# A hybrid decoder layer on one core: the bounded difference of the decays' sums moves from VectorE to ScalarE, and its loads move one chunk forward in the order

## The chip, the cores and the metric

The kernel runs on 1 core of one Trainium2 chip. The metric is the device time in microseconds (us) of the whole kernel. TensorE is called PE below, VectorE DVE, ScalarE ACT, GpSimd POOL, and SyncE, whose queue issues all DMAs, SP.

## The reference, cut to what matters

One layer: an RMSNorm, one input projection for all branches, a differential attention, a gated short convolution and a Mamba-2 scan (SSD), then an output projection and a last RMSNorm. 1024 tokens and 16 meta tokens, model width 1024, all in float32. The change touches the scan alone:

```
adt  = a * dt                                  # per head, 16 heads in 4 groups of R = 4
acum = cumsum(adt) inside a chunk of 128       # "sums of the decays"
seg  = acum[..., :, None] - acum[..., None, :]
lmat = exp(where(causal, seg, -inf))           # 128 x 128 for each head and chunk
y_diag = (C B^T * lmat) @ (x * dt)             # inside the chunk
y_off  = (C @ state) * exp(acum)               # from the chunks before
state  = state * exp(acum[-1]) + B^T (decay_s * x * dt)
```

The kernel forms `lmat` transposed: keys on the 128 partitions, queries along the free axis. It doesn't mask `seg` before the exponential; it bounds the difference at 0 (for a query after the key the difference is never above 0), and the causal triangle is multiplied in afterwards, together with C B^T.

## The kernel before, in words

The work is cut into four iterations, one for each group of heads: the order `BODY` for the first three and `LAST` for the fourth, with a prologue `AHEAD` in front and the output projection behind (from 887 us on). An order is a list of steps with their argument, written by `schedule()` (L185 to L337). Every engine walks the same list and carries out its own part of a step; SP does the DMAs of a step. Nothing else orders the work: each engine runs its instructions in the order of the list, and semaphores hold it back where it needs another engine.

An iteration has an attention part and a scan part. In the scan part the loop of L303 goes over c = 1 to 11. In round c stand, in this order: `chunk c`; `norm c-2`; a fifth of the round's filler; `scan c-1`; `carry c`; `decay c+1`; three fifths of the filler; `ssm_out c-2`; the last fifth. The filler is independent PE work that is dealt over the rounds: steps `project` (PE, 12 matmuls for each half of a piece), `piece` (the copy of a finished piece out of its PSUM bank), `load` (a tile of w_in, by SP), `split` (that tile into a high part by ACT, L991 to L994, and a low part, by POOL at L904 and for a half of two tiles by DVE at L1286), and the short convolution. Pieces use PSUM banks 0 and 1 in turn, so PE can begin piece n+2 only when ACT or DVE has emptied the bank of piece n. The steps `z 1` to `z 8` (PE L1800, 24 matmuls each) use the same two banks: ACT makes a tanh (L1105), DVE multiplies (L1465) and frees the bank. `z 4` stands in front of `chunk 0` and `decay 1`; `z 5` stands in round 1, and `z 6` to `z 8` behind `decay 2`.

What the steps of the scan do:

- `decay a`. SP (L780 to L787) loads the sums of four heads for chunk a, broadcast to all partitions (256 KB), into one of two halves of `acum_b`. It waits until the difference of chunk a-2 is formed (semaphore `seg_ok`), and for a = 1 also for stores of an earlier step. DVE (L1428 to L1435) waits for that load (`acum_in`) and for `scan a-2` (`scan_done`, as the matrices of chunk a-2 lie in the same half of `lm_buf`), and makes four `tensor_scalar` (L1433, 128x128 each: subtract the key's own sum, take the minimum with 0). ACT (L1099 to L1101) waits for `seg_ok` and makes one exponential over 128x512 in place, which counts `l_ok`.
- `chunk a`. PE turns x and B and forms C B^T (L1785). DVE makes x*dt (L1445), x*d (L1448), the masked C B^T (L1451), a copy of B (L1452), and then, once `l_ok` and `scan a-1` are there, the product with `lmat` (L1456, which counts `g_ok`). POOL makes one more product (L919).
- `scan a`. PE: four matmuls with `lmat` (L1814), the part from the state (L1816), the new state (L1820). DVE: state (L1474), three steps of y (L1477 to L1481), the gated y (L1485).
- `norm a` and `ssm_out a`. ACT squares y (L1110), DVE takes the mean (L1492), POOL the power (L895), ACT scales y (L1112), PE turns it (L1584), ACT copies it out (L1119).

In `LAST` the filler also holds `out_load 0` to `3` (SP L792 to L807: two loads each for the output projection). `out_load 0` stands in round 6 and waits until the last tile of w_in is split (`w_lo_ok`, L796); `out_load 1` stands in round 7, in front of `scan 6` and `decay 8`.

Of the kernel before, what the change touches and what calls it, by code (L numbers as in the profile page):

```python
# [11 lines left out]
ALU = mybir.AluOpType  # L12
# [172 lines left out]
def schedule(last):  # L185
    out = []

    def add(name, arg=0, d=0):
        if not (last and d):
            out.append((name, arg, d))  # L190

    def emit(unit):
        for name, arg, d in unit:
            if name in ("load", "split"):
                add(name, arg % NT, d + arg // NT)
            else:
                add(name, arg, d)

    def filler(units, jobs, slots):
        state = [0, 0.0]  # L200

        def fill(weight=1.0):
            state[1] += weight
            while state[0] < len(units) and state[0] < len(units) * state[1] / slots - 1e-9:

                while jobs and jobs[0][0] <= state[0] - 7 and not (last and jobs[0][1][0] == "conv"):
                    emit([jobs.pop(0)[1]])
                emit(units[state[0]])
                state[0] += 1

        def spare(n):
            while n > 0 and jobs and jobs[0][0] <= state[0]:
                emit([jobs.pop(0)[1]])
                n -= 1
        return fill, spare

    units, jobs = half_pieces([TXS0, TXS1, TB, TC, TG], 0)
    fill, spare = filler(units, jobs, sum(ATT_FILL))

    def t_sums(s, at):  # L220

        a, n = divmod(3 * (s - 3) + at, 8)
        if s < 3 or a >= T_PAIRS:
            return
        if n == 0:
            add("t_load", a)
        elif 3 <= n < 7:
            add("t_sum", (a, n - 3))
        elif n == 7:
            add("t_store", a)  # L230

    for s in range(QB + 1):
        f = [ATT_FILL[s] * w for w in (ATT_SPLIT if s < QB else ATT_LAST)]
        if s < QB:
            add("scores", (s, 0))
        fill(f[0])
        t_sums(s, 0)
        if s < QB:
            spare(ATT_SPARE[0])
        if s == 0:  # L240
            add("turn_v")
        if s >= 1:
            add("turn", s - 1)
        if s == QB:
            add("split", TZ1)
            add("load", TCB)
            add("load", TCC)
            add("attn_out", 0)
        if s < QB:
            add("exp", (s, 0))  # L250
        fill(f[1])
        t_sums(s, 1)
        if s < QB:
            add("scores", (s, 1))
            add("exp", (s, 1))
        if s >= 1:
            add("values", s - 1)
        if s == 5:
            add("o_mean", 0)
        if s < QB:  # L260
            spare(ATT_SPARE[1])
        if s < QB:
            add("mix", s)
        if s == 6:
            add("o_scale", 0)
        fill(f[2])
        t_sums(s, 2)
        if s < QB:
            spare(ATT_SPARE[2])

    add("o_mean", 1)
    add("z", 1)
    spare(1)
    add("o_scale", 1)
    add("z", 2)
    spare(2)
    add("z", 3)
    add("attn_out", 1)
    add("store_attn")
    spare(9)  # L280
    add("z", 4)
    add("chunk", 0)
    add("decay", 1)
    units = [[("z", a, 0)] for a in range(5, QB + 1)]
    units[-1].append(("split", TCB, 0))
    units += [[]] * PAUSE
    conv, jobs = half_pieces([TCB, TCC, TCH, TGC], 0)
    jobs = [(n + len(units), job) for n, job in jobs]
    if last:
        for n in range(len(conv)):  # L290
            if ("split", TGC, 0) in conv[n]:
                for j in range(EARLY):
                    conv[n + j].append(("out_load", j, 0))
                conv[-5].append(("out_slot", 0, 0))
                conv[-2].append(("out_slot", 1, 0))
                break
        units += conv
        jobs.pop()
    else:
        units += conv + half_pieces([TQ, TK, TV], 1)[0]  # L300
    slots = LAST_FILL if last else SCAN_FILL
    fill, spare = filler(units, jobs, sum(slots))
    for c in range(1, CH + 3):  # L303
        f = [slots[c - 1] * w for w in SCAN_SPLIT]
        if c < CH:
            add("chunk", c)
        if 1 <= c - 2 < CH:
            add("norm", c - 2)
        if last and c == CH + 1:
            spare(9)  # L310
            for j in range(EARLY, KS):
                add("out_load", j)
            add("conv", 4)
            add("out_slot", 3)
            add("out_slot", 4)
        fill(f[0])
        if not (last and c == CH):
            spare(SCAN_SPARE[0])
        if c - 1 < CH:
            add("scan", c - 1)  # L320
            if 0 < c < CH - 1:
                add("carry", c)
        if c + 1 < CH:
            add("decay", c + 1)
        fill(f[1])
        if not (last and c == CH):
            spare(SCAN_SPARE[1])
        if 1 <= c - 2 < CH:
            add("ssm_out", c - 2)
        fill(f[2])  # L330
        spare(SCAN_SPARE[2])
        if c == CH and last:
            add("out_slot", 2)
            add("out_begin", 0)
    add("store_ssm")
    spare(9)
    return out  # L337
# [46 lines left out]
def build(nc, x, meta_tokens, norm_w, w_in, w_out, attn_lambda, attn_norm_w, sconv_w, ssm_conv_w,  # L384
# [6 lines left out]
    with ExitStack() as ctx:  # L391
# [322 lines left out]
        def _(eng):  # L714
# [24 lines left out]
            def iteration(i, steps):  # L739
                for step, a, d in steps:  # L740
# [36 lines left out]
                    elif step == "conv" and a == 4:  # L777
                        eng.wait_ge(convg_ok, it + 2)
                        eng.dma_start(y_dram[bass.ds(it * P + HEADS * P, P), :], conv_y[:, :]).then_inc(convg_st, 16)
                    elif step == "decay":  # L780

                        eng.wait_ge(seg_ok, it * QB + max(a - 2, 0) + 1)
                        if a == 1:
# [169 lines left out]
        def _(eng):  # L953
# [24 lines left out]
            def iteration(i, steps):  # L978
                for step, a, d in steps:
# [114 lines left out]
                    elif step == "values":  # L1094
# [2 lines left out]
                        eng.wait_ge(o_sq, it * QB + a + 1)  # L1097
                        eng.activation(o_squares, o_n[:, a, :], ACT.Square, accum_out=o_ss[:, a:a + 1]).then_inc(o_sq, 1)
                    elif step == "decay":  # L1099
                        eng.wait_ge(seg_ok, it * QB + a + 1)  # L1100
                        eng.activation(lmat[:, a % 2, :, :], lmat[:, a % 2, :, :], ACT.Exp).then_inc(l_ok, 1)  # L1101
                    elif step == "z":
                        p = PZ + a - 1
                        eng.wait_ge(piece_done, it * PPI + p + 2)
                        eng.activation(th_piece[:, p % 2, 0:GW], pb[p % 2][:, 0:GW], ACT.Tanh, scale=0.5).then_inc(zth_ok, 1)  # L1105
                    elif step == "norm":
                        n = it * QB + a
                        eng.wait_ge(y_gated, n + 1)
                        eng.wait_ge(z_ms_ok, n)
                        eng.activation(th_tile[:, 0:GW], y_n[:, a % 2, :], ACT.Square, accum_out=z_ss[:, a % 2:a % 2 + 1]).then_inc(z_sq, 1)  # L1110
                        eng.wait_ge(z_rs_ok, n)
                        eng.activation(y_n[:, a % 2, :], y_n[:, a % 2, :], ACT.Copy, scale=z_rs[:, a % 2:a % 2 + 1]).then_inc(y_n_ok, 1)  # L1112
                    elif step == "ssm_out":
                        n = it * QB + a
                        eng.wait_ge(y_tr, n + 1)
                        if a == 1:
                            eng.wait_ge(ssm_st, it * 32 + 16)
                        for t in range(2):
                            ins = eng.activation(ys[:, t, (a - 1) * P:a * P], yt_ps[:, t * P:(t + 1) * P], ACT.Copy, scale=par_sn[:, t:t + 1])  # L1119
                        ins.then_inc(ys_ok, 1)  # L1120
                    elif step == "out_slot":
                        if a >= 3:
                            eng.wait_ge(piece_done, HEADS * PPI + 1)
                        slot_free(a)
                        high_y(a)
                        high_w(a)
# [46 lines left out]
        def _(eng):  # L1173
# [18 lines left out]
            def iteration(i, steps):  # L1192
                for step, a, d in steps:
# [218 lines left out]
                    elif step == "conv":  # L1412
# [11 lines left out]
                        else:  # L1424
                            for b in range(2):
                                eng.wait_ge(bank_free[b], it * (PPI // 2) + (PPI + 1 - b) // 2 + 1)
                            eng.scalar_tensor_tensor(conv_y[:, :], conv_y[:, :], 0.5, conv_g[:, META:L], ALU.mult, ALU.mult).then_inc(convg_ok, 1)
                    elif step == "decay":  # L1428

                        eng.wait_ge(acum_in[a % 2], it * 64 + 16 * ((a + 1) // 2))  # L1430
                        eng.wait_ge(scan_done, it * CH + max(a - 1, 0) + 1)
                        for r in range(R):
                            ins = eng.tensor_scalar(lmat[:, a % 2, r, :], acum_b[:, a % 2, r, :], sg[:, 1, a, r:r + 1], 0.0,  # L1433
                                                    ALU.subtract, ALU.min)
                        ins.then_inc(seg_ok, 1)  # L1435
                    elif step == "chunk":

                        n = META if a == 0 else P
# [430 lines left out]
```

## Time and profile before

| | us |
|---|---|
| median of 3 runs (lowest, highest) | 1050.74 (1050.49, 1052.12) |
| the profiled execution: its time | 1049.79 |
| the profiled execution: its span, first to last instruction | 1048.1 |
| PE busy in the span | 1013.8 (97%) |
| DVE busy | 665.6 (64%) |
| ACT busy | 401.8 (38%) |
| POOL busy | 253.8 (24%) |
| scan part of the first head group | about 162 to 275 |
| scan part of the last head group | about 795 to 887 |

The granted clock of PE is 0.998 of full speed over the span. "Busy" counts the time in which an instruction of the engine runs; what is missing to the span is idle time. Of the 16,326 instructions 128 are the four differences of 32 decay steps, and 32 are their exponentials.

### The profile page before, as it was taken

The page shows a single profiled execution, that of the slowest core. Times are in us where ns is not written, and L with a number is a line of the kernel's source. Part 1 is how long each engine was busy: PE and PEld are TensorE (multiplying, and loading weights), DVE is VectorE, ACT ScalarE, POOL GpSimd, SP SyncE. Part 2 cuts the span into 40 slices and gives each one's busy share as a digit, 9 for nine tenths or more (in the row PEclk, how much of TensorE's full clock was granted, in tenths as well). Part 3 has the DMA queues.
Part 4 walks back from the last instruction along what each step waited for, and adds up shares of the span by engine and source line. Part 5 has one row for each costly group of instructions (what it writes and reads, how often), then busy time and mean ns, then how long its engine had stood idle before and what let it go on. Part 6 is the DMA issues. An engine that isn't in the chain of part 4 may idle for free.

```text
span 1048.1 us, 16326 instructions
## 1 busy us (share of the span) xinstructions
PE 1013.8 (97%) x6177; PEld 924.9 (88%) x6177; DVE 665.6 (64%) x1327; ACT 401.8 (38%) x892; POOL 253.8 (24%) x222
## 2 busy tenths in 40 slices
PE   4999999999999999999999999999999999999996
PEld 3889989898999898989999989899999898888885
DVE  7555767557257674672576756724767646798866
ACT  6333442233444332334343222343442233544554
POOL 3012331333223312332224133222241330000002
PEclk9999999999999999999999999999999999999999
DMA  8012322221142222211422322114223203994313
GB/s 268 1 44 81 101 81 71 71 61 44 47 133 101 71 81 71 61 41 41 141 84 76 93 71 61 42 41 141 76 70 101 71 20 105 359 389 140 100 51 161
DMA packets 105945, 101.22 MB, mean 97 GB/s; under 512 B 6022, under 2 KB 79852, under 8 KB 105868
## 3 DMA queue, kind: packets, MB, share of 16 engines
q1 hardware_dynamic: 105868, 100.18, 30.0%
q8 instruction: 50, 0.82, 0.3%
q14 instruction: 27, 0.22, 0.1%
HBM read 79.11 MB, written 21.05 MB: 96 GB/s over the span
## 4 chain that ended last, share of the span: by engine, by line
PE 84%; DVE 7%; issue 3%; DMA 2%; ACT 2%; POOL 1%; SPq 0%; POOLq 0%; DVEq 0%; ACTq 0%
PE ps L1599 43%; PE ps L1608 13%; PE ps L1800 9%; PE ps L1584 5%; PE ps L1765 3%; DVE lm_buf L1433 2%; PE ps L1814 2%; DMA acum_b<-acum_scratch 2%; PE ps L1743 2%; PE ps L1744 2%; PE ps L1816 1%; PE ps L1820 1%; PE ps L1691 1%; PE ps L1766 1%; DMA conv_u<-in_norm_w 1%
## 5 line engine op out<-in xcount | busy, mean ns | idle before, releaser
L1599 PE MATMUL ps<-u_hi,w_hi 128*128 128x348 f32 (+3 forms) x1024 | 364.4, 356 | 6.7 <-ACT conv_b_s L1053 2.5
L1599 PE MATMUL ps<-u_lo,w_hi 128*128 128x348 f32 (+3 forms) x1024 | 348.3, 340 | 0.0
L1599 PE MATMUL ps<-u_hi,w_lo 128*128 128x348 f32 (+3 forms) x1024 | 347.7, 340 | 0.0
L1599 PEld LDWEIGHTS ps<-u_hi,w_hi 128*128 128x128 f32 x1024 | 194.0, 189 | 19.8 <-issue 5.5
L904 POOL TENSOR_TENSOR w_lo<-w_raw,w_hi 128x1024 fp32r<-128x1024 f32 (+1 forms) x56 | 123.1, 2197 | 346.2 <-ACT w_hi L994 274.4
L1599 PEld LDWEIGHTS ps<-u_hi,w_lo 128*128 128x128 f32 x1024 | 193.3, 189 | 10.9
L1599 PEld LDWEIGHTS ps<-u_lo,w_hi 128*128 128x128 f32 x1024 | 193.7, 189 | 10.3
L895 POOL TENSOR_TENSOR small<-small,m_half 128x1 f32<-128x1 f32 (+2 forms) x57 | 41.5, 729 | 338.9 <-DVE small L1545 144.8
L1372 DVE TENSOR_REDUCE small<-ps 128x1 f32<-128x144 f32 (+7 forms) x64 | 49.5, 774 | 95.8 <-PE ps L1747 95.3
L1800 PE MATMUL ps<-w_hi,u_hi 128*128 128x256 f32 x256 | 73.1, 286 | 0.0
L1800 PE MATMUL ps<-w_lo,u_hi 128*128 128x256 f32 x256 | 72.0, 281 | 0.0
L1800 PE MATMUL ps<-w_hi,u_lo 128*128 128x256 f32 x256 | 72.0, 281 | 0.0
L1086 ACT ACTIVATE work<-ps,small 128x144 f32<-128x144 f32 (+7 forms) x64 | 48.0, 751 | 53.7 <-DVE small L1372 53.7
L1584 PE MATMUL ps<-ident,work 128*128 128x128 f32 (+2 forms) x369 | 56.6, 288 | 6.1 <-DVE work L1208 6.1
L1608 PE MATMUL ps<-q_hl 128*128 128x512 f32 x264 | 62.1, 389 | 0.0
L1433 DVE TENSOR_SCALAR lm_buf<-acum_b,sg 128x128 f32<-128x128 f32 x128 | 44.5, 409 | 27.5 <-DMA acum_b<-acum_scratch 27.5
L1101 ACT ACTIVATE lm_buf<-lm_buf 128x512 f32<-128x512 f32 x32 | 20.2, 632 | 107.0 <-DVE lm_buf L1433 107.0
L1112 ACT ACTIVATE y_n<-y_n,small 128x256 f32<-128x256 f32 x32 | 16.3, 510 | 112.9 <-POOL small L895 112.9
L1608 PEld LDWEIGHTS ps<-q_hl 128*128 128x128 f32 x264 | 49.6, 188 | 10.3
L1584 PEld LDWEIGHTS ps<-ident,work 128*128 128x128 f32 (+2 forms) x369 | 44.4, 143 | 9.9 <-DVE work L1208 7.8
L1456 DVE TENSOR_TENSOR lm_buf<-lm_buf,cbm 128x512 f32<-128x512 f32 x32 | 22.6, 707 | 43.3 <-PE ps L1820 43.1
L994 ACT CAST w_hi<-w_raw 128x1024 fp32r<-128x1024 f32 x48 | 49.9, 1040 | 0.1
(302 smaller groups left out, 1768.7 us busy)
## 6 DMA issues: line engine op xcount, KB each, us to landing
w_raw<-in_w_in SPq DMA_DIRECT2D x56, 512.0 KB, 4.1
acum_b<-acum_scratch SPq DMA_DIRECT2D x32, 256.0 KB, 4.4
acum_b<-in_w_out SPq DMA_DIRECT2D x22, 256.0 KB, 4.3
work<-in_w_out SPq DMA_DIRECT2D x16, 256.0 KB, 4.0
t_scratch<-work SPq DMA_DIRECT2D x16, 256.0 KB, 2.3
t_scratch<-acum_b SPq DMA_DIRECT2D x16, 256.0 KB, 2.6
y_scratch<-ys SPq DMA_DIRECT2D x8, 512.0 KB, 4.0
work<-in_x SPq DMA_DIRECT2D x4, 1024.0 KB, 8.4
```

The costliest lines, as they stand in the source:

```text
L895: return eng.tensor_tensor(to[0:rows_, n:n + w], of[0:rows_, n:n + w], m_half[0:rows_, 0:w], ALU.pow)
L904: eng.tensor_tensor(w_lo[:, a % 2, ks, :], w_raw[:, a % 2, ks, :], w_hi[:, a % 2, ks, :].bitcast(F32), ALU.subtract).then_inc(w_lo_ok, 1)
L994: eng.copy(w_hi[:, b, :, :], w_raw[:, b, :, :]).then_inc(w_hi_ok, 1)
L1086: eng.activation(prob[m][:, 0:nk], s_ps[:, 0:nk], ACT.Exp, bias=mx[:, m:m + 1], accum_out=psum_e[:, s % 2, m:m + 1]).then_inc(exp_ok, 1)
L1372: eng.tensor_reduce(mx[:, m:m + 1], s_ps[:, 0:nk], AX.X, ALU.max, negate=True).then_inc(max_ok, 1)
L1433: ins = eng.tensor_scalar(lmat[:, a % 2, r, :], acum_b[:, a % 2, r, :], sg[:, 1, a, r:r + 1], 0.0, ALU.subtract, ALU.min)
L1456: eng.tensor_tensor(lmat[:, b, :, :], lmat[:, b, :, :], cbm[:, b, :].unsqueeze(1).to_broadcast([P, R, P]), ALU.mult).then_inc(g_ok, 1)
L1584: return eng.transpose(dst, src, ident[0:n, 0:n])
L1599: ins = eng.matmul(dst, w[:, k, 0:m], u[:, k, cols], start=(k == 0 and n == 0), stop=(k == KD - 1 and n == 2))
L1608: ins = eng.matmul(ps[:, BANKS[n // KS][t], :], y[:, at], w, start=(begins and m == 0), stop=(ends and m == 2), skip_group_check=True)
L1765: eng.matmul(o_ps[:, P:2 * P], a_t[:, n, :], v_blk[:, n, :], start=(n == 0), stop=False)
L1800: ins = eng.matmul(pb[p % 2][:, 0:GW], u[:, k, ca:cb], w[:, :, k, :], start=(k == 0 and n == 0), stop=(k == KD - 1 and n == 2))
```

## The change

The step `decay` is cut in two. Its load becomes a step `decay_load`, which only SP carries out, with the same waits. Loads 1 and 2 stand in front of `z 4`; load c+1 stands at the head of round c, from c = 2 to 7, in front of `chunk c` and of all the round's filler. So load a stands in front of the filler of round a-1 instead of behind its first fifth and behind `scan a-2`.

The four differences become ACT's. The sums' load and `scan a-2` are now waited for by ACT; it makes four activations `relu(sum of the key - sum of the query)`, with the key's sum as a bias for each partition and a scale of -1, counts `seg_ok`, waits for it, and the exponential takes a scale of -1. DVE has no part in `decay` any more. Number and size of the loads stay as they were, and so does everything else in the list.

```diff
@@ schedule()
     add("store_attn")
     spare(9)
+    add("decay_load", 1)
+    add("decay_load", 2)
     add("z", 4)
     add("chunk", 0)
     add("decay", 1)
...
     for c in range(1, CH + 3):
         f = [slots[c - 1] * w for w in SCAN_SPLIT]
+        if 1 < c and c + 1 < CH:
+            add("decay_load", c + 1)
         if c < CH:
             add("chunk", c)
@@ SyncE
-                    elif step == "decay":
+                    elif step == "decay_load":
 
                         eng.wait_ge(seg_ok, it * QB + max(a - 2, 0) + 1)
@@ ScalarE
                     elif step == "decay":
+                        eng.wait_ge(acum_in[a % 2], it * 64 + 16 * ((a + 1) // 2))
+                        eng.wait_ge(scan_done, it * CH + max(a - 1, 0) + 1)
+
+                        for r in range(R):
+                            ins = eng.activation(lmat[:, a % 2, r, :], acum_b[:, a % 2, r, :], ACT.Relu, bias=sg[:, 1, a, r:r + 1], scale=-1.0)
+                        ins.then_inc(seg_ok, 1)
                         eng.wait_ge(seg_ok, it * QB + a + 1)
-                        eng.activation(lmat[:, a % 2, :, :], lmat[:, a % 2, :, :], ACT.Exp).then_inc(l_ok, 1)
+                        eng.activation(lmat[:, a % 2, :, :], lmat[:, a % 2, :, :], ACT.Exp, scale=-1.0).then_inc(l_ok, 1)
@@ VectorE
-                    elif step == "decay":
-
-                        eng.wait_ge(acum_in[a % 2], it * 64 + 16 * ((a + 1) // 2))
-                        eng.wait_ge(scan_done, it * CH + max(a - 1, 0) + 1)
-                        for r in range(R):
-                            ins = eng.tensor_scalar(lmat[:, a % 2, r, :], acum_b[:, a % 2, r, :], sg[:, 1, a, r:r + 1], 0.0,
-                                                    ALU.subtract, ALU.min)
-                        ins.then_inc(seg_ok, 1)
```

## Rows read from the trace of the kernel before

**Rows 1.** The page: busy time (share of the span) and count of each engine.
```profile
PE 1013.8 (97%) x6177; PEld 924.9 (88%) x6177; DVE 665.6 (64%) x1327; ACT 401.8 (38%) x892; POOL 253.8 (24%) x222
```

**Rows 2.** First scan's window: length, busy us of PE, PEld, DVE, ACT, POOL, clock, DMA.
```profile
162.00:275.00 113.00, 110.84 (x703) 102.40 (x703) 68.56 (x161) 35.65 (x81) 31.73 (x31) 1.00 0.23 66
```

**Rows 3.** Waits of PE, whole span: total us, times, longest.
```profile
PE ps L1599 <- ACT conv_b_s L1053: 2.5, 3, 0.9
PE ps L1599 <- ACT conv_u L1057: 2.4, 3, 0.8
...
PE ps L1599 <- DVE conv_g L1337: 1.2, 3, 0.4
PE ps L1584 <- ACT y_n L1112: 1.2, 2, 1.0
PE ps L1814 <- DVE lm_buf L1456: 0.7, 1, 0.7
PE ps L1599 <- DVE conv_u L1334: 0.5, 1, 0.5
```

**Rows 4.** The chain of waits, first head group: start us, us, what.
```profile
197.60 4.65 DMA acum_b<-acum_scratch
...
203.71 0.58 ACT conv_b_s L1053
...
211.13 3.40 DVE lm_buf L1433 x4
...
215.56 2.16 PE ps L1599 x12
...
244.70 3.40 DVE lm_buf L1433 x4
```

**Rows 5.** Timeline of ACT, first group: start, us, engine, line [idle before it <- releaser].
```profile
196.30 1.04 ACT L994 CAST w_hi<-w_raw 128x1024 fp32r<-128x1024 f32 x1
...
210.26 1.04 ACT L994 CAST w_hi<-w_raw 128x1024 fp32r<-128x1024 f32 x1
...
225.40 0.62 ACT L1119 ACTIVATE ys<-ps,par_sn 128x128 f32<-128x128 f32 x2 [0.29 <-PE ps L1584]
```

**Rows 6.** Line 1433: ns of one (min/median/max), first and last start.
```profile
L1433 DVE TENSOR_SCALAR lm_buf<-acum_b,sg x128: 273/279/2432, 177.2 to 873.0; 128x128 f32<-128x128 f32 x128
```

**Rows 7.** Timeline of POOL, first head group.
```profile
211.37 2.48 POOL L904 TENSOR_TENSOR w_lo<-w_raw,w_hi 128x1024 fp32r<-128x1024 f32 x1 [1.56 <-ACT w_hi L994]
...
225.19 2.38 POOL L904 TENSOR_TENSOR w_lo<-w_raw,w_hi 128x1024 fp32r<-128x1024 f32 x1 [3.63 <-ACT w_hi L994]
```

**Rows 8.** Groups of ACT: busy us, mean ns of one | idle before them, releaser.
```profile
L1101 ACT ACTIVATE lm_buf<-lm_buf 128x512 f32<-128x512 f32 x32 | 20.2, 632 | 107.0 <-DVE lm_buf L1433 107.0
L1119 ACT ACTIVATE ys<-ps,par_sn 128x128 f32<-128x128 f32 x64 | 20.0, 367 | 14.8 <-PE ps L1584 14.8
...
L1112 ACT ACTIVATE y_n<-y_n,small 128x256 f32<-128x256 f32 x32 | 16.3, 510 | 112.9 <-POOL small L895 112.9
L1110 ACT ACTIVATE th_tile<-y_n 128x256 f32<-128x256 f32 x32 | 13.5, 422 | 0.1
```

**Rows 9.** Timeline of ACT, last group: the shortest idle time before an exponential.
```profile
850.22 0.63 ACT L1101 ACTIVATE lm_buf<-lm_buf 128x512 f32<-128x512 f32 x1 [1.35 <-DVE lm_buf L1433]
```

**Rows 10.** Timeline of DVE, first group, around the z steps.
```profile
177.25 0.88 DVE L1433 TENSOR_SCALAR lm_buf<-acum_b,sg 128x128 f32<-128x128 f32 x4 [1.97 <-DMA acum_b<-acum_scratch]
...
179.82 0.41 DVE L1465 SCALAR_TENSOR_TENSOR work<-th_piece,ps 128x256 f32<-128x256 f32 x1
```

**Rows 11.** The chain of waits, first group: three z steps of PE.
```profile
178.23 8.72 PE ps L1800 x72
```

**Rows 12.** The chain of waits, last group: queue of SP and the last load.
```profile
863.68 0.42 SPq L737
...
865.32 7.09 DMA acum_b<-acum_scratch
```

**Rows 13.** Groups of ACT by form: the only table load of the trace.
```profile
L1000 ACT ACT_TABLE_LOAD x1 | 1.3, 1283 | 0.8 <-PEq L1857 0.8
```

## The prediction

> **What bounds the kernel now.** I read the page's busy line first: PE is busy for 1013.8 of 1048.1 us [rows 1]. No work of another engine counts unless it makes PE wait. The change touches the four scan parts, so the window of the first of them comes next: PE lacks 113.00 - 110.84 = 2.16 us there [rows 2]. Third, the list of PE's waits says who ends such waits [rows 3]: once in each of the first three groups the copies L1053 (2.5 us for the three), L1057 (2.4) and L1337's gating (1.2), 6.1 together; in the last group y_n twice (1.0 and 0.2), L1456 once (0.7) and L1334 once (0.5), 2.4 together. That is 8.5 us in all, and a change that leaves PE's own work alone can't save more in these parts.
>
> Fourth, the chain of waits says what stood behind the copies [rows 4]. The copies themselves are short; they are queued behind the exponential of a decay step on ACT, and that waits for DVE's four differences. At the first place the differences wait for their own load: SP had been held by a load of w_in, and issued the load of the sums only behind it, at 197.60; that took 4.65 us, and the copy ended at 203.71 + 0.58 = 204.29. At the other two places the load is there, but the four differences take 3.40 us in place of 0.88 [rows 4, 10]: one of them took up to 2.432 us where the median is 0.279 [rows 6], and the row of 211.13 to 214.53 lies across POOL's L904 (211.37 to 213.85) [rows 7].
>
> **The change, part by part.**
>
> *The differences leave DVE.* 128 instructions go. Four take 0.88 us where four medians would be 1.12, so neighbours overlap by 0.08, and DVE's chain loses 0.80 us at each decay step [rows 6, 10], or 3.3 us beside L904.
>
> *They are added to ACT.* No 128x128 activation with a pointer that reads SBUF stands in the rows. L1110 has 256 columns without a pointer, 0.422 us; L1101 has 512, 0.632 [rows 8]: 0.210 us for 256 columns, so 128 columns are 0.317. A pointer costs 0.088 (L1112 against L1110, 0.510 against 0.422), which gives 0.40 us each. Two L1119 in a row (0.367 each) took 0.62 [rows 5, 8], so neighbours overlap by 0.11. Four: 4 x 0.40 less 3 x 0.11 = 1.27 us. The bounds: not below the 0.88 of DVE's four, since L1119, the nearest row, is slower than L1433; not above 4 x 0.632 = 2.53, the exponential with four times the columns. I take 1.27, from the near rows. The exponential keeps its 0.63. ACT's wait on its own count I put at nothing to 0.1 us, and inside the rounding.
>
> *What this does to ACT's order.* ACT stood idle before the exponentials for 107.0 us [rows 8], before each of the 32, 1.35 us at the least [rows 9]. It now waits itself for the load and for `scan a-2`, and both are older than DVE's result, since DVE did L1456, L1474 and the steps up to L1485 between that scan and the differences. So the 1.27 us lie in idle time, and an exponential starts earlier than before, at the tightest place by 0.08 us. Behind the waiting ACT are queued the tanh of z, the copies of pieces and the squares; all of them waited for the exponential before too.
>
> One place is late: `decay 1`, where the load arrives last (DVE waited 1.97 us for it, until 177.25 [rows 10]). There ACT's four cost 1.27 instead of 0.88, and what follows is 0.4 us later: behind the exponential DVE makes L1456 and frees the bank of `z 5`, at 179.82 + 0.41 = 180.2 before [rows 10]. PE wants that bank for `z 7`, a third of the way into its row of three, at 178.23 + 2.91 = 181.1 [rows 11]. A margin of 0.9 shrinks to 0.5: nothing is lost. DVE gains there, as it no longer stands still for the load.
>
> *The three places.* First: ACT was free at 196.30 + 1.04 = 197.34 [rows 5]. Load 4 lies there by then: its gate, the difference of `decay 2`, opens near 181, and SP meets it before the held load of w_in. So the exponential ends near 199.3 and the copy near 199.9. PE wants the bank about 0.9 before it began, near 203.5: 3.6 us to spare, and the wait goes whole. Second: ACT was free at 210.26 + 1.04 = 211.3 [rows 5]; 1.27 + 0.63 more gives 213.2, the copy (at most the other's 0.58) ends by 213.8, and PE wants it at 215.56 - 0.8 = 214.8 [rows 3, 4]: 1.0 to spare. Third: DVE's four took 3.40 us from 244.70 [rows 4]; ACT's 1.27 start no later, so the exponential and L1337 behind it come at least 2.1 us earlier, against a wait of 0.4 [rows 3]. All 6.1 us go. Late next are the bank of the second place (1.0 us) and that of `z 7` (0.5).
>
> *The last group.* The 1.0 us wait for y_n has DVE's four in its chain, without the stretch: 0.80 comes off, 0.2 stays. The 0.7 for L1456 has no decay step in its chain (w_in's split, then `chunk 2`) and stays, and so does the second wait for y_n, 0.2. The 0.5 for L1334 stood behind DVE's wait for the last load (865.32, 7.09 us [rows 12]) and goes, since DVE doesn't wait any more. But the load itself is hardly ahead: load 8 stands at the head of round 7, and `out_load 0`, in round 6, holds SP until the last tile of w_in is split. SP then issues two loads for it, the second at 863.68 [rows 12], and load 8 at about 864.1, 1.2 us earlier than before, in a crowd. ACT waits for it until 869 to 871 (the 4.65 to 7.09 us that such loads took), ends the exponential near 871 to 873, and PE wants the y_n behind it about 876: covered. Sum here 0.80 + 0.5 = 1.3 us.
>
> *The other loads.* SP carries the same 32 loads. Each now stands in front of a round's loads of w_in and could hold these, but its gate, the difference of a-2, is two rounds old. I put this at nothing; the cover is the time from a w_in load, issued next to 197.60 and some 5 us under way, to its split at 210.26 [rows 4, 5], 8 us. Loads that land earlier gain no more than the waits counted above.
>
> *The sum.* 6.1 + 1.3 = 7.4 us. For the profiled execution: span 1048.1 - 7.4 = 1040.7, time 1049.79 - 7.4 = 1042.4. The median of the runs lies 0.95 above the profiled time, so I expect 1050.74 - 7.4 = 1043.3 us.
>
> *Where rules of the skill bear on it.* That a stretched difference ran beside POOL's L904 is in the rows; that it is a lock is not. The Trainium skill (SBUF — State Buffer, on its engine and DMA ports) says that VectorE and GpSimd share one port pair, that one instruction holds it whole while the other stands still, and that ScalarE has ports of its own. By it ACT's four keep their length beside L904 and the sum stands at 7.4 us; without it the first rival holds, at 3.8. ACT's L1119 at 225.40 took 0.62 for two beside POOL's L904 of 225.19 [rows 5, 7], so by that rule the trace agrees.
>
> The same skill speaks against the move (ScalarE: Activation LUTs, Rules for kernel authors): relu, max and min are VectorE's, not ScalarE's. The rows agree so far as 0.40 us stand against 0.279; what it would do here is the fourth rival.
>
> **The rivals.**
>
> *1. The stretch follows the work.* If what stretches L1433 is traffic in memory and not a matter between DVE and POOL, ACT's four stretch too. The second place has them at 211.3, just as L904 starts (211.37 to 213.85 [rows 7]): they end near 214.9 and the copy near 216, so PE waits as before, and so at the third place. Gone are then the first place's 2.5 us [rows 3] and the last group's 1.3: 1050.7 - 3.8 = 1046.9. Against it is L1119 beside L904.
>
> *2. The waits come back elsewhere.* Drawn together, PE could meet the z banks (0.5 us of margin), y_n or the state late, and gain nothing: 1050.7. For it: the chain of y_n runs over DVE, POOL and ACT, and already costs 0.2 and 1.0. Against it: that chain starts at PE's own `scan`, so it moves forward along with PE, and DVE loses work.
>
> *3. Slower: relu isn't in the table set of the exponential.* The trace has one table load in all, 1.283 us [rows 13]; squares, exponentials, tanh and copies alternate without one, but relu isn't among them. If it forces a reload, a decay step has two, 2.57 us more, and every place with less margin decides against the change: the bank of `z 7` (0.5) comes 2.1 us late, that behind the second decay about as late again, the second place (1.0) 1.6, the third (2.1 less 0.4) 0.9. That is some 6.5 us in each of four groups, 26 us, with the 7.4 gone: 1069. Against it is the mixture above.
>
> *4. Slower: ACT's chain is on the path everywhere.* 1.27 against 0.88 in 32 steps is 12.5 us: 1063. Against it are the 1.35 us or more of idle time before each exponential.
>
> **How the numbers follow.** Forecast 0.76, first rival 0.12, second 0.07, third 0.03, fourth 0.02. The median of this kernel's runs tells 0.2%, 2.1 us, from no change. Faster is the forecast and the first rival, 0.88; same is the second, 0.07; slower 0.05. The predicted time is the forecast's, 1043.3. Below it the bound is the 8.5 us: 1042.2, and about half a us for the scatter of medians, 1041.6. Above it the first rival's 1046.9 is taken in, with the same scatter and a little: 1047.6. The upper bound of ACT's four (2.53, 1.26 more than taken) would cost 0.8 us in the z steps of each group and 0.3 at the second place, some 4 us: 1047.3, inside.
>
> **What would show each step.** L1433 gone from DVE; four new activations of 0.37 to 0.40 us at each of 32 places, a row of four in 1.2 to 1.3 us, also beside L904. PE's waits for L1053, L1057 and L1337 gone; those for y_n down to 0.4 in all; L1456's 0.7 still there. Loads 2 to 8 landed before ACT wants them, but for load 8 of the last group, issued behind two loads of `out_load 0`, where ACT waits for 3 to 6 us. One table load. The prediction is wrong if PE's missing time in the four scan parts isn't down to about 1.1 us in all, or if an exponential starts later than before at any place but `decay 1`.

## The result, and the profile after

The changed kernel takes 1040.2 us (median of 4 runs, 1040.0 to 1041.1), the kernel before in the same comparison 1050.88 (1050.49 to 1052.12): a ratio of 0.9895, with a 95% interval of 0.9881 to 0.9909. In a later comparison it stood at 1040.92 against 1050.17, 0.9913 (0.9900 to 0.9927). So the gain is 9.3 to 10.7 us. Forecast were 7.4 us, with 1041.6 as the lower end of the range: the direction was right, and the time lies below the range. Two executions among the experiments below, one of the kernel with ScalarE alone and one of that with load 8 ahead, took 2026 and 3550 us: the ratios leave them out, and without them these two medians are 1045.45 and 1040.67 instead of 1045.52 and 1040.9.

The profiled execution has a span of 1038.7 us, against 1048.1. Its busy line answers to [rows 1]:

```profile
PE 1010.6 (97%) x6177; PEld 923.9 (89%) x6177; DVE 623.7 (60%) x1199; ACT 443.3 (43%) x1020; POOL 253.9 (24%) x222
```

DVE lost 42 us and 128 instructions, and ACT gained the same 128 and 41.5 us. Look at PE: the same 6177 instructions, but 3.2 us less busy time. The prediction counted on PE's idle time alone, so this is the first sign of what it missed; it is taken up below.

PE's waits (total, times, longest), which answer to [rows 3]. The one for `work`, 1.2 us longer than before in this execution, belongs to the prologue, and so do two more of 8.6 and 2.3 us. The copies L1053 and L1057 (now L1057 and L1061), the wait for L1337 and that for L1334 are gone, y_n is down from 1.2 to 0.4, and L1456 (now L1458) keeps its 0.7, as forecast:

```profile
PE ps L1586 <- DVE work L1218: 7.3, 4, 2.6
...
PE ps L1816 <- DVE lm_buf L1458: 0.7, 1, 0.7
PE ps L1586 <- ACT y_n L1122: 0.4, 2, 0.2
```

The window of the first scan, for [rows 2] (columns as there). PE lacks nothing any more:

```profile
162.00:273.00 111.00, 111.00 (x710) 103.06 (x709) 57.54 (x130) 46.47 (x114) 32.27 (x31) 1.00 0.23 67
```

ACT's differences, from the view of their line (ns of one: min, median, max; then what ended ACT's idle time before them):

```profile
L1108 ACT ACTIVATE lm_buf<-acum_b,sg x128: 384/389/408, 177.9 to 860.4; 128x128 f32<-128x128 f32 x128
its engine sat idle before it (us, times) until:
  DMA acum_b<-acum_scratch: 15.1, 6
  PE ps L1822: 3.8, 4
```

And the second place of the prediction, ACT's timeline, with POOL's split beside it (210.83 to 213.23):

```profile
209.72 1.04 ACT L998 CAST w_hi<-w_raw 128x1024 fp32r<-128x1024 f32 x1
210.65 1.28 ACT L1108 ACTIVATE lm_buf<-acum_b,sg 128x128 f32<-128x128 f32 x4
211.96 0.64 ACT L1111 ACTIVATE lm_buf<-lm_buf 128x512 f32<-128x512 f32 x1
212.50 0.42 ACT L1061 COPY conv_u<-ps 128x342 f32<-128x342 f32 x1
```
```profile
210.83 2.40 POOL L908 TENSOR_TENSOR w_lo<-w_raw,w_hi 128x1024 fp32r<-128x1024 f32 x1 [1.56 <-ACT w_hi L998]
```

Four in 1.28 us (1.27 forecast), not stretched beside POOL, where DVE's four took 3.40 [rows 4].

**Where the time came from.** The best clock in this kernel is the start of the same PE work in each head group. These are the first three z steps of each group, in the chain of waits (start us, us, what), and the start of the output projection's steady part. First before, then after:

```profile
162.09 8.51 PE ps L1800 x72
...
373.12 8.51 PE ps L1800 x72
...
584.01 8.51 PE ps L1800 x72
...
794.87 8.52 PE ps L1800 x72
...
895.55 130.63 PE ps L1608 x576
```
```profile
162.72 8.52 PE ps L1802 x72
...
370.85 8.53 PE ps L1802 x72
...
578.97 8.52 PE ps L1802 x72
...
787.07 8.52 PE ps L1802 x72
...
886.15 130.63 PE ps L1610 x576
```

From group to group it was 211.03, 210.89 and 210.86 us, and is 208.13, 208.12 and 208.10: 8.43 us less. From the last group's z steps to the output projection it was 100.68 and is 99.08: 1.60 less. Together 10.03 us. Behind that point both take 152.55 us. In front of it the changed kernel's prologue took 0.63 us longer in this execution. The change doesn't touch the prologue, but over the executions shown here its end lies anywhere from 161.8 to 163.6, and a whole time moves with it. The distances don't: in a second trace of the changed kernel they are 208.10, 208.15, 208.12 and 99.05. So the experiments below are read by distances first. The change itself is worth 10.0 us; the idle time that left PE's list is 7.4 (8.5 less 1.1).

The same stretch, from the first group's z steps to the output projection, in the view by windows (columns as in [rows 2]), before and after:

```profile
162.09:895.55 733.46, 724.65 (x4649) 673.86 (x4648) 445.21 (x944) 258.22 (x607) 205.72 (x170) 1.00 0.25 76
```
```profile
162.72:886.15 723.43, 722.07 (x4649) 673.12 (x4648) 403.59 (x816) 299.49 (x735) 205.72 (x170) 1.00 0.25 77
```

PE's idle time falls from 8.81 to 1.36 us, by 7.45, and its busy time by 2.58 for the same 4649 matmuls. The other 0.6 of the page's 3.2 us lie in the prologue.

### The profile page after: what moved, and what is told of

Read it like the earlier page. It is cut to its first block, busy times and chain, and to the rows that moved or that the text cites. A ratio compares the mean times of both kernels' runs of the same rounds, so it can differ in the third digit from the quotient of the medians.

```text
span 1038.7 us, 16326 instructions
## 1 busy us (share of the span) xinstructions
PE 1010.6 (97%) x6177; PEld 923.9 (89%) x6177; DVE 623.7 (60%) x1199; ACT 443.3 (43%) x1020; POOL 253.9 (24%) x222
## 4 chain that ended last, share of the span: by engine, by line
PE 93%; DVE 3%; issue 1%; ACT 1%; DMA 1%; POOL 0%; POOLq 0%; SPq 0%; DVEq 0%; ACTq 0%
PE ps L1601 51%; PE ps L1610 13%; PE ps L1802 9%; PE ps L1586 5%; PE ps L1767 3%; PE ps L1816 2%; PE ps L1745 2%; PE ps L1746 2%; PE ps L1818 1%; PE ps L1822 1%; PE ps L1693 1%; PE ps L1768 1%; PE ps L1787 1%; DMA conv_u<-in_norm_w 1%; PE ps L1749 0%
## 5 line engine op out<-in xcount | busy, mean ns | idle before, releaser
L1458 DVE TENSOR_TENSOR lm_buf<-lm_buf,cbm 128x512 f32<-128x512 f32 x32 | 22.1, 691 | 50.8 <-PE ps L1822 40.4
L1802 PEld LDWEIGHTS ps<-w_hi,u_hi 128*128 128x128 f32 x256 | 48.1, 188 | 1.3 <-issue 1.3
L1108 ACT ACTIVATE lm_buf<-acum_b,sg 128x128 f32<-128x128 f32 x128 | 40.8, 391 | 19.0 <-DMA acum_b<-acum_scratch 15.1
```

Of the source, the lines that this page charges most:

```text
L1108: ins = eng.activation(lmat[:, a % 2, r, :], acum_b[:, a % 2, r, :], ACT.Relu, bias=sg[:, 1, a, r:r + 1], scale=-1.0)
L1458: eng.tensor_tensor(lmat[:, b, :, :], lmat[:, b, :, :], cbm[:, b, :].unsqueeze(1).to_broadcast([P, R, P]), ALU.mult).then_inc(g_ok, 1)
L1802: ins = eng.matmul(pb[p % 2][:, 0:GW], u[:, k, ca:cb], w[:, :, k, :], start=(k == 0 and n == 0), stop=(k == KD - 1 and n == 2))
```

## The experiments

The open question: 10.0 us came from waits that the trace gave as 7.4. **Theory:** a wait costs PE more than the idle time shown, since matmuls in a row overlap, and a wait takes that overlap away too. Compare the first place in both traces, the timeline of PE (start, us, line; an entry of several is merged), first before and then after:

```profile
203.10 0.39 PE L1785 MATMUL ps<-work 128*128 128x128 f32 x2
204.42 0.39 PE L1599 MATMUL ps<-u_hi,w_hi 128*128 128x342 f32 x1 [0.94 <-ACT conv_b_s L1053]
```
```profile
203.74 0.39 PE L1787 MATMUL ps<-work 128*128 128x128 f32 x2
203.88 0.40 PE L1601 MATMUL ps<-u_hi,w_hi 128*128 128x342 f32 x1
```

From start to start it is 1.32 us with the wait and 0.14 without: 1.18 us lost, where the trace says 0.94 idle. The other 0.24 stand in it as busy time.

**Rival A:** a wait costs its idle time, and the 2.6 us come from elsewhere. **Rival B:** they come from DVE's lighter load.

### One part at a time: the loads alone

```diff
 # the kernel before, with the change's schedule() and SP step
-                    elif step == "decay":          # SyncE
+                    elif step == "decay_load":
 # ScalarE and VectorE as before
```

> The kernel before with the loads of the sums moved forward alone; the differences stay on VectorE. Theory (a wait of PE costs its idle time in the trace and about 0.24 us more, as the start-to-start distances of the two traces say): the waits for L1053 go (3 x (0.85 + 0.24)) and that for L1334 (0.5 + 0.24), those for L1057 and L1337 stay, since the differences still lie across POOL's L904: 4.0 us, about 1046.8. Rival A (a wait costs its idle time and no more): 3.0 us, 1047.8. Rival B (the excess over the idle time came from VectorE's lighter load): 3.0 us here too, and the excess turns up in the kernel that moves the differences alone.

Measured: 1046.83 us against 1050.33 beside it, ratio 0.9966 (0.9955 to 0.9978). That interval is 1045.6 to 1048.0 us, so it holds the theory's 1046.8 and the rivals' 1047.8 alike, and the traces have to decide. PE's waits that are left in the scan:

```profile
PE ps L1603 <- ACT conv_u L1061: 2.4, 3, 0.8
...
PE ps L1603 <- DVE conv_g L1341: 1.3, 3, 0.4
PE ps L1588 <- ACT y_n L1116: 1.2, 2, 1.0
PE ps L1818 <- DVE lm_buf L1460: 0.7, 1, 0.7
```

The step between two groups is 209.87 us (373.45 to 583.32) against 210.89: 1.02 us for one wait of about 0.8 [rows 3]. Over the three groups (163.55 to 793.18) it is 3.15 us for waits of 2.5, so 0.22 more for each of the three, and with the last group 3.99 us, against 4.0 by the theory and 3.0 by the rivals. Both rivals fall here: the excess is there, though DVE's load didn't become lighter. The loads alone bring 40% of the 10.0 us.

### The other part: ScalarE alone

```diff
 # the changed kernel
-    add("decay_load", 1)
-    add("decay_load", 2)
     add("z", 4)
     add("chunk", 0)
+    add("decay_load", 1)
     add("decay", 1)
...
-        if 1 < c and c + 1 < CH:
-            add("decay_load", c + 1)
...
         if c + 1 < CH:
+            add("decay_load", c + 1)
             add("decay", c + 1)
```

> The changed kernel with the loads put back to where they stood, directly in front of the differences, which ScalarE makes. Theory: the waits for L1057 (3 x (0.8 + 0.24)), L1337 (3 x (0.4 + 0.24)), L1334 (0.5 + 0.24) and 0.8 of y_n go; the waits for L1053 stay and grow by 0.4 each, as ScalarE's four are that much longer behind the landed load: 5.4 us in all, about 1045.4. Rival A: 3.3 + 1.2 to 1.3 - 1.2, about 3.7 us, 1047.1. Rival B: 2.3 us more than rival A, 1044.8, and none of it in the first experiment.

Measured: 1045.52 us, ratio 0.9953 (0.9940 to 0.9966), 0.1 us from the theory's number (rival B's was 1044.8, rival A's 1047.1). The interval is 1044.0 to 1046.8 us: it leaves out rival A's number, but not rival B's. By the distances the gain is 3.97 us in three groups and 1.08 in the last, 5.05 together, against 5.4 by the theory and 3.7 by rival A. What is missing lies with y_n, which kept 0.8 us in three waits where 0.4 in two was expected. The wait for the copy L1053 stayed and grew from 2.5 to 3.7 for the three, by 0.4 each:

```profile
PE ps L1599 <- ACT conv_b_s L1055: 3.7, 3, 1.6
```

The two parts alone bring 3.5 and 4.8 us by their medians, 4.0 and 5.05 by the distances, and both together 10.0. Each takes waits that the other leaves, and only both together take away the late load without putting ACT's slower four behind it.

### What a wait costs: 28 waits for PE's own matmuls, and their control

```diff
 # the changed kernel, TensorE; the control waits for x_done instead of scan_done
+                    elif step == "carry":
+                        eng.wait_ge(scan_done, it * CH + a + 1)
```

> The changed kernel, and PE waits for the end of its own scan matmuls in every carry step, 28 times, before it goes on with matmuls that need nothing of them. Theory: each wait costs what lies between the usual start of the next matmul (0.35 us before the modelled end of the last one, which is 0.59 us for two of 256 columns) and the end with its signal, 0.40 to 0.45 us, of which the trace shows only 0.1 or less as idle time: 11 to 12.5 us, 1051 to 1053, with PE's missing time up by 3 us at the most. Rival A: the time grows by no more than the idle time shown, 3 us, 1043.

> The control of the drained wait: the same 28 waits at the same places, but on a count that the chunk step's matmuls gave a microsecond earlier, so the wait is met already. Theory: the pipeline isn't drained, 0 to 0.5 us, 1040.2 to 1040.7. Rival C (the wait instruction itself costs, drained or not): as much as the drained one, 1051 or more.

Measured: 1048.17 us with the drained waits, 1040.08 with the control. A wait that is met costs nothing that can be measured (rival C falls). From group to group it is 210.14 us (161.81 to 371.95) against 208.12 (162.05 to 370.17), 0.29 for each of seven, and 6.02 us for the 21 of three groups, again 0.29. In the last group it is only 1.15 us for seven, but there the two waits for y_n (0.4) are gone and L1456's is down from 0.7 to 0.4: the drained waits took their place. That the medians also differ by 28 x 0.29 = 8.1 us is chance in part, since the distances sum to 7.2. I had expected 0.40 to 0.45: I took the later start of one matmul for the cost, but the matmul behind it follows closer. The pages' busy lines decide between the theory and rival A, first the drained waits, then the control:

```profile
span 1044.9 us, 16340 instructions
...
PE 1017.4 (97%) x6177; PEld 922.3 (88%) x6177; DVE 623.5 (60%) x1199; ACT 442.7 (42%) x1020; POOL 253.5 (24%) x222
```
```profile
span 1038.0 us, 16340 instructions
...
PE 1011.3 (97%) x6177; PEld 924.3 (89%) x6177; DVE 623.8 (60%) x1199; ACT 442.7 (43%) x1020; POOL 253.5 (24%) x222
```

The span is 6.9 us longer with the same 6177 matmuls. Of that 6.1 (1017.4 less 1011.3) are shown as busy and 0.8 as idle. In the first group alone, where no other wait is mixed in, 1.61 of the 2.02 us are busy time and 0.41 idle: 0.23 and 0.06 for each wait. Rival A falls: of so short a wait the trace books four fifths as busy. One place, first with the drained wait, then in the control:

```profile
206.95 0.59 PE L1822 MATMUL ps<-xdd,b_n 128*128 128x256 f32 x2
207.60 0.42 PE L1601 MATMUL ps<-u_hi,w_hi 128*128 128x342 f32 x1
207.87 0.32 PE L1601 MATMUL ps<-u_lo,w_hi 128*128 128x342 f32 x1
```
```profile
206.50 0.59 PE L1822 MATMUL ps<-xdd,b_n 128*128 128x256 f32 x2
206.75 0.51 PE L1601 MATMUL ps<-u_hi,w_hi 128*128 128x342 f32 x1
207.09 0.32 PE L1601 MATMUL ps<-u_lo,w_hi 128*128 128x342 f32 x1
```

The next matmul starts 0.65 us after the scan's pair instead of 0.25, and 0.06 us of it is idle time; the one behind it starts 0.92 us after the pair instead of 0.59. The Trainium skill describes such a thing (TensorE: Matmul & The Clock Gate, Step-by-step: what each phase is for): the drain of one matmul runs under the fill of the next, and only a stream hides it. The trace agrees in kind; that it is the drain and nothing else that costs here, no run shows. The size is taken from these runs. What a wait costs above its idle time, by the distances:

| what differs | waits | us by distances | us idle | more for each |
|---|---|---|---|---|
| loads ahead, three groups | 3 | 3.15 | 2.5 | 0.22 |
| POOL's split cut short as well (next section) | 6 | 5.22 | 3.7 | 0.25 |
| the whole change, three groups | 9 | 8.43 | 6.1 | 0.26 |
| drained waits against their control, first group | 7 | 2.02 | 0.41 | 0.23 |

### Is it POOL that stretches DVE's differences?

```diff
 # the first experiment's kernel (loads ahead, differences on VectorE), GpSimd
                         ks = slice(KD // 2 if a in SHARED or step == "split_low" else 0, KD)
+                        if steps is not AHEAD and (a > TCB or d == 1):
+                            ks = slice(0, 1)
```

> The first experiment's kernel (loads ahead, differences on VectorE), and POOL makes only an eighth of the low parts of the w_in tiles that are split in the scan: L904 there is short, and those parts of the result are left out. Theory (L1433 is stretched by POOL's L904 and by nothing else, and that is what the copies L1057 and the wait for L1337 cost): no L1433 over 0.5 us, these two waits gone, 3 x (0.8 + 0.25) + 3 x (0.4 + 0.25) = 5.1 us less than the first experiment, about 1041.7, and 208.1 us from one head group to the next instead of 209.9. Rival (VectorE's own work stretches the chain): 209.9 stays, 1046.8.

Measured: 1041.09 us, ratio 0.9911 (0.9898 to 0.9925), and 208.12 us between groups (370.98 to 579.10), as in the changed kernel. The waits for L1057 and L1337 are gone. With that rival B falls for the whole change as well: DVE still makes the differences here and is busy for 655.5 us, against 623.7 in the changed kernel, and the three groups take the same time. Line 1433's instruction, first in the kernel with the loads ahead, then here:

```profile
L1437 DVE TENSOR_SCALAR lm_buf<-acum_b,sg x128: 272/280/2433, 178.3 to 867.5; 128x128 f32<-128x128 f32 x128
```
```profile
L1439 DVE TENSOR_SCALAR lm_buf<-acum_b,sg x128: 273/281/668, 177.7 to 859.9; 128x128 f32<-128x128 f32 x128
```

So the stretch comes from POOL's L904, and without it DVE could have made the differences in time. In the first three groups the move to ACT gained by leaving POOL's neighbourhood, not by DVE's load. The last group is another matter: y_n keeps its 1.2 us of waits here and has 0.4 in the changed kernel, so those 0.8 come from taking the four out of DVE's chain. The maximum is 668 ns and not under 500 as expected: where it occurs (a row of four took 1.45 us from 418.84), POOL ran the cut instruction (0.56 us from 419.08) and another one of its own (0.61 from 419.60). The kernel leaves work out, so it isn't a version to use.

### Two more on the last group

First, load 8 of the last group in front of `out_load 0`:

```diff
 # the changed kernel; the round's own load is left to c + 1 < CH - last
+            if (name, arg) == ("out_load", 0):
+                add("decay_load", CH - 1)
```

> The changed kernel with load 8 of the last group in front of out_load 0, so that it isn't held any more. Theory (that wait of ScalarE is covered): ScalarE's wait of 2.7 us before the differences of decay 8 goes, PE waits as before, 1040.1 within 0.4. Rival (the wait for the last load is on PE's path after all): 1 us or more faster.

Measured: 1040.9 us, a ratio of 0.9904 (0.9889 to 0.9920), between the changed kernel's 0.9895 and 0.9913. It isn't within the 0.4 us expected, but the distance that the load could change is the same: 99.06 us from the last z steps to the output projection, against 99.08. ACT's differences followed y_n at once, where in the changed kernel ACT had stood idle for 2.70 us; first here, then there:

```profile
857.21 1.27 ACT L1110 ACTIVATE lm_buf<-acum_b,sg 128x128 f32<-128x128 f32 x4
```
```profile
859.47 1.28 ACT L1108 ACTIVATE lm_buf<-acum_b,sg 128x128 f32<-128x128 f32 x4 [2.70 <-DMA acum_b<-acum_scratch]
```

The wait was covered. Second, a try at the waits that are left there:

```diff
 # the changed kernel
-    units += [[]] * PAUSE
+    units += [[]] * (2 if last else PAUSE)
```

> The changed kernel with 2 empty places in the last group's filler instead of 4, so that half a piece stands in front of scan 2 and another in front of ssm_out 1, as in the first three groups. Theory (three waits are left in the last group, 0.7 + 0.2 + 0.2 us of idle time, each with 0.25 us that the trace counts as busy): 1.3 to 1.8 us faster than the changed kernel, about 1038.5. Rival A (idle time only): 0.7 to 1.1, 1039.2. Rival D (other waits open in their place): 1040.1 or more.

Measured: 1044.71 us, ratio 0.9942 (0.9929 to 0.9954), 4 us slower than the changed kernel where 1.3 to 1.8 faster was forecast: rival D held. The 0.7 for L1456 did go, but two larger waits came:

```profile
PE ps L1586 <- ACT y_n L1122: 2.0, 4, 1.4
PE ps L1601 <- DVE w_lo L1296: 2.0, 1, 2.0
```
```profile
859.87 0.51 ACT L1122 ACTIVATE y_n<-y_n,small 128x256 f32<-128x256 f32 x1 [3.09 <-POOL small L899]
867.46 1.28 ACT L1108 ACTIVATE lm_buf<-acum_b,sg 128x128 f32<-128x128 f32 x4 [7.08 <-DMA acum_b<-acum_scratch]
```

`z 8` had moved behind `chunk 2`, and with it the split that stands behind it, so its low part came too late for the half piece, 2.0 us at 817.7. And load 8 now stood behind two of `out_load`, so ACT waited 7.08 us for it and y_n came late for PE, by 1.4 us. The cover of the last load had been real, and thin. PE's idle time in this list is 4.0 us against 1.1, and there are two waits more: 2.9 + 0.5 = 3.4 us. The distance from the last z steps to the output projection says the same, 102.45 us against 99.08, 3.37 more. The edit also shifts the half pieces in most later rounds, so that these two steps are the causes is read from the trace, and no run changed one of them alone. The version that keeps the z steps in place and has load 8 ahead (its clause for round 6 makes up for that for round 3, and the order of all other rounds stays):

```diff
 # the kernel with load 8 ahead
-        f = [slots[c - 1] * w for w in SCAN_SPLIT]
+        f = [slots[c - 1] * w for w in ((.8, .2, 0.) if last and c == 3 else (.2, .8, 0) if last and c == 6 else SCAN_SPLIT)]
```

> The kernel with load 8 ahead, and in the last group alone round 3 gets the order that it has in the first three groups: load 12, split 11 and half a piece in front of scan 2, the other half in front of ssm_out 1. All z steps stay where they were. Theory: the wait for L1456 (0.7 + 0.25) and the first one for y_n (0.2 + 0.25) go, the second for y_n stays: 1.4 us less than the changed kernel beside it, with no new wait as in the kernel with 2 empty places, where z 8 had come behind chunk 2. Rival D (the filler that is taken from round 3's later part is missed at another place): no gain, or a loss.

> The changed kernel itself, beside the last experiment on the same chip: 1040.2 within 0.5 us by every theory.

Measured beside each other: 1039.23 and 1040.92 us (ratios to before 0.9897, 0.9883 to 0.9910, and 0.9913, 0.9900 to 0.9927). The gain of 1.7 us is near the 1.4 forecast, and by the distance from the last z steps to the output projection, 97.72 us against 99.05, it is 1.33. The changed kernel itself, expected at 1040.2 within 0.5, came out 0.2 beyond that. The intervals overlap, but no run of the one (at most 1039.47) reaches a run of the other (at least 1040.26), and rival D falls. One of the scan's waits is left:

```profile
PE ps L1588 <- ACT y_n L1124: 0.2, 1, 0.2
```

It is the fastest version that was run.

## Why the prediction was wrong

- **The term that failed** is the saving itself. The prediction said "8.5 us in all, and a change that leaves PE's own work alone can't save more in these parts", and put 6.1 + 1.3 = 7.4 us on waits that go. It took a wait's idle time for its cost, and so put what a wait costs above it at nothing, without a reason. Ten waits went altogether (nine in the first three groups and L1334), each with 0.22 to 0.26 us that the trace books as busy: with 0.25, 7.4 + 2.5 = 9.9, against 10.03 by the starts. In the trace it is the 2.58 us of PE's busy time that went beside the 7.45 us of idle time. By the same account the bound was 8.5 + 13 x 0.25 = 11.75, and not 8.5, and the lower end of the range, which rested on that bound, was too high.
- **The mechanism held.** All of the first three groups' waits went, y_n kept 0.2 + 0.2, and L1456 kept 0.7, as forecast. PE's missing time in the scan parts is down to 1.1 us, and no exponential but `decay 1`'s starts later, so neither of the two signs that the prediction named for being wrong came up, though the time left its range. Of the two parts alone, the corrected account gave the first to 0.01 us and the second to 0.35, by the distances; that both medians lay within 0.1 us of their forecasts is luck, as the kernel before measured 1050.33 beside them and not the 1050.8 that they started from.
- **ACT's four**: 0.389 us each and 1.28 for the row, against 0.40 and 1.27. The way by two nearby forms and the difference of a pointer was good to 3%.
- **`decay 1`**: in the first group the exponential starts 0.4 us later (16.5 us after the first z step instead of 16.1), as forecast; in the others it is 0.6, 0.4 and 0.2. The z banks took no harm: PE's row of three takes 8.72 us as before.
- **The loads**: forecast were loads 2 to 8 in time but for the last. Load 5 of the last group was 1.3 us late too, as it stood behind a load of w_in there; and ACT's wait for load 8 was 2.7 us and not 3 to 6. PE's list has no wait behind either, and the run with load 8 ahead shows it for load 8.
- **The rivals.** The stretch that follows the work fell by the trace (1.28 beside POOL), and the kernel with short low parts says that POOL's L904 makes it. That the waits come back elsewhere fell too, but it is what happened to the version with 2 empty places. There was one table load, as before, so the third falls. The fourth falls as well: counted from the z steps of its group, no exponential but `decay 1`'s starts later.

## What to carry to other kernels

In a kernel like this one, where PE runs without a break but for a few short waits, price each wait at its idle time plus a quarter of a us, and don't take the idle time of a profile as the most that can be had. Measure by the distance from the start of the same work in one loop to its start in the next: it repeated to 0.05 us here, and it doesn't depend on where the profile puts the end of a matmul. Before moving an operation off an engine because it is slow at one place, look at what runs beside it there: it may be the neighbour. And a load that is moved ahead in one queue is ahead only if nothing in front of it holds the queue.

## What the runs showed of the hardware that was not expected

- A wait of PE for its own last matmuls costs 0.29 us, of which 0.06 are shown as idle (0.41 of 2.02 us in seven). The same wait on a count that is there already, 3 us earlier at the place shown, costs nothing that can be measured (208.12 us from group to group against 208.13, and 1040.08 against 1040.2 and 1040.92).
- A DVE `tensor_scalar` of 0.28 us took up to 2.43 beside POOL's subtraction of 2.4 us, and 0.67 at most where that was cut short, while ACT's 128 activations, some of them beside it, took 0.384 to 0.408.
